# Hybrid RG-LRU layer on one core: the lead-in taken by pairs of contraction tiles, with all eight x_lru tiles in it

## The chip, the core and the metric

One core of a Trainium2 chip runs the whole kernel. Its engines work side by side and meet through semaphores: PE (TensorE) multiplies matrices, DVE (VectorE) and ACT (ScalarE) do elementwise work, POOL (GpSimd) and SP (SyncE) here mostly issue DMA transfers. The metric is device time in microseconds (us), lower is better. Matrix operands lie in SBUF with 128 partitions; products are summed in PSUM, which has eight banks of 512 float32 columns.

## The reference

One layer with two streams, 128 context tokens and 256 latent tokens, which the kernel carries together as T = 384 columns; D = 2048, LRU width 1024, eight heads of 128.

```python
m   = silu(cvec) @ w_mod + b_mod                 # six vectors of 2048: shift, scale, gate, shift, scale, gate
hn  = rmsnorm(x, g[0]) * (1.0 + mod[:, 1]) + mod[:, 0]
z   = hn @ w_in                                  # x_lru | y_gate | b_g | c_g | v, 1024 columns each
xc  = dwconv(x_lru, cw, (2, 1)) + cb             # four taps
o_f, s_f = rglru_dir(xc, ..., reverse=False)     # gates: block-diagonal 128x128 products, then a scan
o_b, s_b = rglru_dir(xc, ..., reverse=True)
lru_out = (o_f + o_b) * gelu(y_gate)
sc_out  = b_g * dwconv(c_g * v, sc_w, (1, 1))
x = x + mod[:, 2] * (concat(lru_out, sc_out) @ w_out)
hn = rmsnorm(x, g[1]) * (1.0 + mod[:, 4]) + mod[:, 3]
x = x + mod[:, 5] * ((silu(hn @ w_gate) * (hn @ w_up)) @ w_down)
```

The outputs are both streams after a final RMSNorm and the last states of the context scans.

## The kernel before, in words

Every float32 product is made of three matmuls of rounded operands (`product`): high activation by high weight, low activation by high weight, high activation by low weight. ACT rounds a weight block to its high part, DVE subtracts to get the low part, and four slots (`w_hi`, `w_lo`) hold such blocks. Weights arrive through four raw buffers `raw` of 1 MB. A contraction tile `k` is one of the 16 groups of 128 input channels; `KT` is 16.

The lead-in is what has to happen before `hn @ w_in` can run at full depth:

- **Rows of w_mod.** Shift and scale together are 4096 columns of `w_mod`. PE multiplies them with the two conditioning vectors in rows of 512 columns: four units of 1 MB each (`lead_matmuls`), summed in `MOD_BANK`. DVE copies a row to `mod_row` (`copy_lead_row`), PE turns it into columns (`turn_lead_row`), DVE adds the bias (`add_lead_bias`). Before, a row holds either the shift or the scale of four contraction tiles: rows 0, 2, 4 are shift, rows 1, 3, 5 scale. The last four tiles have one shift row and two scale rows of two tiles each (256 columns), nine rows in all (`LEAD_ROWS`). Only after both rows can four tiles be scaled.
- **Activations.** With 1/rms known (`make_rstd`), DVE makes the normalized tiles of a pair (`hat_pair`), DVE and ACT scale and shift the context and latent columns (`scale_ctx`, `norm_pair`), ACT rounds to `act_hi`, DVE makes `act_lo` (`low_act`).
- **x_lru in the lead-in.** SP loads, for each `k`, the first 768 columns of `w_in` (`load_x_weights`, two buffers `x_raw`); ACT and DVE split them (`round_x`, `subtract_x`). `x_product` is half of one `k`: three of six output tiles, each summed over all 16 `k` in a PSUM bank of its own (`X_BANKS`). The halves stand between the units of the later rows.
- **After it.** The other two x_lru tiles are a step of four blocks (`N_X3`, 4 us of PE each) with four of the units of a further w_mod row behind its blocks (`mod_units`). ACT copies finished x_lru tiles into `padded` (`pad_tile`), DVE convolves them (`convolve_x`), some of them in this step and the rest in the first of eight steps of `gm_step`, which also hold the gates of one head each (`head_gates`). Each step has eight blocks of eight products.
- **SP's order** is one queue: a w_mod unit waits until the matmuls have freed its raw buffer (`mod_used`), an x weight load until the low part made from its buffer is there (`lo_ready`). A load that waits holds up all loads behind it.

The instruction order of each engine is the order of the code; nothing is scheduled by a planner. `decays()` is a chain of 17 small DVE instructions on the decay parameters, placed between low parts 2, 3 and the first row of the loop over fours.

Of the kernel before, what the change touches and what calls it, by code (L numbers as in the profile page):

```python
# [23 lines left out]
ALU = mybir.AluOpType  # L24
# [4 lines left out]
P = 128  # L29
SLOTS = 4  # L30
# [33 lines left out]
def build(nc, x_prompt, x_sample, state_rglru, c, c_ctx, w_mod, b_mod, norm_g, w_in, lru_conv_w, lru_conv_b,  # L64
# [65 lines left out]
    N_X3 = KT  # L130
    N_IN = N_X3 + 4
    N_OUT = N_IN + (IN_STEPS - 2) * 8
    MOD_IN, MOD_OUT = MOD_FIRST + 1, MOD_FIRST + IN_STEPS - 1
    assert MOD_STEPS - MOD_FIRST == 1 + (IN_STEPS - 2) + OUT_STEPS + 3 and len(LEAD_UNITS) == 4 * MOD_FIRST
# [11 lines left out]
    with ExitStack() as ctx:  # L146
# [52 lines left out]
        x_squares = [lru[:, b] for b in (2, 3)]  # L199
        x_sumsq = scratch[:, 8 * T:10 * T].rearrange("p (a t) -> p a t", a=2)  # L200
# [4 lines left out]
        x_raw = [scratch[:, at:at + X_WIDE] for at in (4 * P + 8 * 2 * HEADS, 8 * T + 4 * PADDED + 2 * T - X_WIDE)]  # L205
        POS = GRID_ROWS * (KT // 2) + GRID_W * (KT // 2)
        pos = scratch[:, 8 * T + 2 * T:8 * T + 2 * T + POS]
# [7 lines left out]
        X_BANKS = (2, 3, 0, 1, 4, 5)  # L215
# [60 lines left out]
        x_pair_done = sem("x_pair_done")  # L276
        squared = sem("squared")
# [70 lines left out]
        def landings(kind, n, block):  # L348

            if kind in ("GM", "GX"):  # L350
                return X_LANDED + 16 * (block // 4 + 1) + 4 * (n - N_X3)
            earlier = 0 if block // 2 % 2 else 4 * (N_G1 - N_X3)
            return X_LANDED + earlier + 16 + 2 * (n - N_G1)

        X_LANDED = 16 * MOD_FIRST
# [59 lines left out]
        def gains_before(pair):  # L415

            return sum(1 for first, _ in LEAD_ROWS if KT <= first <= KT + 2 * pair)

        def lead_unit(row, unit):

            number = LEAD_UNITS.index((row, unit))
            slot = number % SLOTS
            width = P * LEAD_ROWS[row][1]
            return slot, 16 * (number // SLOTS + 1), raw[slot][:].rearrange("p (k n) -> p k n", n=width)
# [5 lines left out]
        def _(sp):  # L430
# [26 lines left out]
            def load_lead_unit(number):  # L457

                row, unit = LEAD_UNITS[number]
                first, tiles = LEAD_ROWS[row]  # L460
# [1570 lines left out]
```

## Time and profile before

| what | value |
|---|---|
| runs | 1747.32 us median of 3 (1746.41 to 1747.57) |
| profiled execution | span 1746.0 us from first to last instruction; its own total is not shown apart from that |
| PE busy | 1712.1 us, 98% of the span |
| DVE busy | 945.4 us, 54% |
| ACT busy | 610.0 us, 35% |
| HBM read | 303.55 MB, 176 GB/s over the span |

The lead-in is in the first 4 of 40 slices of 43.65 us of the page. PE is busy 5 tenths of the first slice and 9 or more of every other but the last. The DMA row reads 9, 9, 9, 6 there, and 3 to 8 in nearly all later slices. "PEclk" or "granted clock" is the TensorE clock in parts of full speed: 1.00 is 2.4 GHz and 0.50 is 1.2 GHz. A busy interval of a matmul holds its fill and drain, and neighbours overlap; how fast a stream runs is read from the distance between starts.

### The profile page before, as it was taken

The page shows a single profiled execution, that of the slowest core. Times are in us where ns is not written, and L with a number is a line of the kernel's source. Part 1 is how long each engine was busy: PE and PEld are TensorE (multiplying, and loading weights), DVE is VectorE, ACT ScalarE, POOL GpSimd, SP SyncE. Part 2 cuts the span into 40 slices and gives each one's busy share as a digit, 9 for nine tenths or more (in the row PEclk, how much of TensorE's full clock was granted, in tenths as well). Part 3 has the DMA queues.
Part 4 walks back from the last instruction along what each step waited for, and adds up shares of the span by engine and source line. Part 5 has one row for each costly group of instructions (what it writes and reads, how often), then busy time and mean ns, then how long its engine had stood idle before and what let it go on. Part 6 is the DMA issues. An engine that isn't in the chain of part 4 may idle for free.

```text
span 1746.0 us, 24522 instructions
## 1 busy us (share of the span) xinstructions
PE 1712.1 (98%) x10063; PEld 1634.1 (94%) x10063; DVE 945.4 (54%) x1405; ACT 610.0 (35%) x701; POOL 63.6 (4%) x99
## 2 busy tenths in 40 slices
PE   5999999999999999999999999999999999999997
PEld 3678999999999979999999999999999999999997
DVE  4447578777778578353535444353534435353445
ACT  3233555456522253223232322223222232223235
POOL 2000100110010110000000000000000000000000
PEclk8999999999999999999999999999999999999998
DMA  9996755676677876343334333433343334333421
GB/s 364 388 349 223 247 200 199 205 241 205 212 256 260 280 265 220 130 134 121 120 128 136 120 120 127 137 120 120 127 137 120 120 126 138 120 120 126 138 73 73
DMA packets 206269, 307.56 MB, mean 176 GB/s; under 512 B 5501, under 2 KB 151217, under 8 KB 203777
## 3 DMA queue, kind: packets, MB, share of 16 engines
q1 hardware_dynamic: 189472, 237.07, 40.5%
q0 software_dynamic: 16528, 69.63, 11.2%
q8 instruction: 43, 0.70, 0.2%
q14 instruction: 18, 0.14, 0.0%
q10 hardware_dynamic: 208, 0.02, 0.0%
HBM read 303.55 MB, written 3.15 MB: 176 GB/s over the span
## 4 chain that ended last, share of the span: by engine, by line
PE 93%; DMA 4%; DVE 1%; ACT 1%; SPq 0%; issue 0%; ACTq 0%; DVEq 0%
PE psum L1590 30%; PE psum L1591 29%; PE psum L1592 29%; DMA raw<-in_w_mod 2%; DMA scratch<-in_w_in 2%; PE psum L1620 1%; PE psum L1612 1%; PE psum L1634 1%; PE psum L1928 0%; PE psum L1645 0%; PE psum L1699 0%; ACT scratch L668 0%; DVE act_lo L1143 0%; DVE w_lo L1121 0%; SPq L465 0%
## 5 line engine op out<-in xcount | busy, mean ns | idle before, releaser
L971 DVE TENSOR_TENSOR w_lo<-raw,w_hi 128x1024 fp32r<-128x1024 f32 x364 | 444.1, 1224 | 643.3 <-ACT w_hi L633 642.9
L1590 PE MATMUL psum<-act_hi,w_hi 128*128 128x384 f32 x2240 | 753.8, 337 | 3.1 <-DVE act_lo L1143 2.3
L1592 PE MATMUL psum<-act_hi,w_lo 128*128 128x384 f32 x2240 | 750.2, 335 | 0.0
L1591 PE MATMUL psum<-act_lo,w_hi 128*128 128x384 f32 x2240 | 750.0, 335 | 0.0
L633 ACT ACTIVATE w_hi<-raw 128x1024 fp32r<-128x1024 f32 x364 | 381.6, 1058 | 790.9 <-PE psum L1592 717.1
L1590 PEld LDWEIGHTS psum<-act_hi,w_hi 128*128 128x128 f32 x2240 | 421.1, 188 | 26.3 <-issue 17.5
L1591 PEld LDWEIGHTS psum<-act_lo,w_hi 128*128 128x128 f32 x2240 | 421.3, 188 | 0.0
L1592 PEld LDWEIGHTS psum<-act_hi,w_lo 128*128 128x128 f32 x2240 | 421.2, 188 | 0.0
L1590 PE MATMUL psum<-h_hi,w_hi 128*128 128x384 f32 x768 | 258.3, 336 | 0.9 <-DVE h_lo L1450 0.9
L1592 PE MATMUL psum<-h_hi,w_lo 128*128 128x384 f32 x768 | 257.0, 335 | 0.0
L1591 PE MATMUL psum<-h_lo,w_hi 128*128 128x384 f32 x768 | 256.9, 335 | 0.0
L1590 PEld LDWEIGHTS psum<-h_hi,w_hi 128*128 128x128 f32 x768 | 144.2, 188 | 6.2 <-issue 5.0
L1591 PEld LDWEIGHTS psum<-h_lo,w_hi 128*128 128x128 f32 x768 | 144.3, 188 | 0.0
L1592 PEld LDWEIGHTS psum<-h_hi,w_lo 128*128 128x128 f32 x768 | 144.2, 188 | 0.0
L1459 DVE SCALAR_TENSOR_TENSOR xT<-psum,modT,xT 128x128 f32<-128x128 f32 x352 | 122.0, 409 | 6.8 <-PE psum L1592 6.7
L992 DVE SCALAR_TENSOR_TENSOR token_rows<-raw,cond,token_rows 128x512 f32<-128x512 f32 x90 | 61.6, 745 | 0.0
L1634 PE MATMUL psum<-raw,cond_w 128*32 128x512 f32 (+1 forms) x288 | 36.9, 602 | 5.7 <-DMA raw<-in_w_mod 5.6
L992 DVE SCALAR_TENSOR_TENSOR scratch<-stage,cond,scratch 128x512 f32<-128x512 f32 x62 | 42.4, 745 | 0.0
L870 ACT ACTIVATE h_hi<-stage 128x768 fp32r<-128x768 f32 x22 | 18.6, 847 | 51.6 <-DVE stage L1445 51.6
L827 ACT ACTIVATE scratch<-xT 128x768 f32 (+1 forms) x8 | 6.8, 847 | 77.7 <-DVE xT L1387 77.7
L1121 DVE TENSOR_TENSOR w_lo<-scratch,w_hi 128x768 fp32r<-128x768 f32 x16 | 15.1, 955 | 28.7 <-ACT w_hi L654 28.7
L654 ACT ACTIVATE w_hi<-scratch 128x768 fp32r<-128x768 f32 x16 | 13.3, 838 | 41.2 <-DMA scratch<-in_w_in 41.2
(191 smaller groups left out, 760.5 us busy)
## 6 DMA issues: line engine op xcount, KB each, us to landing
raw<-in_w_mod POOLq DMA_DIRECT2D x50, 1024.0 KB, 6.0
raw<-in_w_gate SPq DMA_DIRECT2D x44, 1024.0 KB, 5.0
raw<-in_w_up SPq DMA_DIRECT2D x44, 1024.0 KB, 5.0
raw<-in_w_down SPq DMA_DIRECT2D x44, 1024.0 KB, 4.9
raw<-in_w_in SPq DMA_DIRECT2D x34, 1024.0 KB, 5.3
raw<-in_w_mod SPq DMA_DIRECT2D x32, 1024.0 KB, 9.6
raw<-in_w_out SPq DMA_DIRECT2D x16, 1024.0 KB, 5.5
stage<-in_w_mod POOLq DMA_DIRECT2D x14, 1024.0 KB, 7.5
```

The lines of the kernel that those rows point to most:

```text
L633: act.activation(split_view(w_hi, b), source, ACT.Copy).then_inc(hi_ready, 1)
L870: act.activation(h_hi[:, 2 * pair:2 * pair + 2, :], silu_g[:, 2 * pair:2 * pair + 2, :], ACT.Copy)\
L971: dve.tensor_tensor(split_view(w_lo, b), source, split_view(w_hi, b).bitcast(F32), ALU.subtract).then_inc(lo_ready, 1)
L992: dve.scalar_tensor_tensor(sums[:, a, :], rows[:, j, :], cond[:, a, k:k + 1], sums[:, a, :], ALU.mult, ALU.add).then_inc(side_step, 1)
L1121: dve.tensor_tensor(w_lo[k % SLOTS][:, 0:X_WIDE], x_raw[k % 2], w_hi[k % SLOTS][:, 0:X_WIDE].bitcast(F32), ALU.subtract).then_inc(lo_ready, 1)
L1459: last = dve.scalar_tensor_tensor(xT[:, k, start:end], psum[:, down_banks[j] + a, start:end], modT[:, 5 * KT + k, seg:seg + 1], xT[:, k, s ...
L1590: pe.matmul(psum[:, bank, 0:T], hi, x_hi, start=first, stop=False)
L1591: pe.matmul(psum[:, bank, 0:T], hi, x_lo, start=False, stop=False)
L1592: return pe.matmul(psum[:, bank, 0:T], lo, x_hi, start=False, stop=last)
L1612: out = pe.matmul(psum[32 * j:32 * j + 32, MOD_BANK, :], cond_w[:, k, :], rows[:, 512 * j:512 * j + 512], start=k == 0, stop=k == KT - 1, ...
L1620: out = pe.matmul(psum[32 * j:32 * j + 32, MOD_BANK, :], cond_w[:, 4 * q + j, :], rows[:, j, :], start=q == 0, stop=q == 3, tile_position= ...
L1634: out = pe.matmul(psum[32 * j:32 * j + 32, MOD_BANK, 0:tiles * P], cond_w[:, depth * unit + i, :], rows[:, i, :], start=unit == 0 and i < ...
```

## The change

- **Rows.** There are eight rows of 512 columns; row r holds the shift of tiles 2r and 2r+1 in its first 256 columns and their scale in its last 256. Each 1 MB unit is now loaded by two DMAs of 512 KB, whose runs in HBM are 256 columns (1 KB) where they were 512 columns (2 KB). One row makes one pair of tiles ready.
- **x_lru.** All eight tiles are in the lead-in: 1024 columns of `w_in` for each `k`. Tiles 0 to 3 are summed over all `k` in banks 0 to 3 (`held_products`). Tiles 4 to 7 are summed in banks 4 and 5 over the two `k` of a pair only (`part_products`), and DVE adds each result to a sum in SBUF (`add_part`, 32 times; it copies in the first pair). The step `N_X3` is gone.
- **Order.** A row's four units stand together on PE, then two part products of the pair before, the turn of the row, and the rest of the pair's products. The convolutions and the first gates move into the first `gm_step`: `head_gates(0, 0)` and two mod units come after its block 1.
- **Loads.** The first row's units are issued ahead of the first two x weight loads. Scratch buffers move accordingly.

```diff
+    X_TILES = HEADS
+    X_HELD = X_TILES // 2
+    LEAD_COUNT = KT // 2
+    X_PART_BANKS = (4, 5)
...
+            def load_lead_unit(row, unit):
+                if row:
+                    sp.wait_ge(mod_used, 4 * row + unit - 3)
+                for s in range(2):
+                    at = s * D + 2 * P * row
+                    sp.dma_start(lead_unit(unit)[:, :, 2 * P * s:2 * P * s + 2 * P],
+                                 w_mod_v[:, 4 * unit:4 * unit + 4, at:at + 2 * P]).then_inc(landed[unit], 16)
...
+            for row in range(1, LEAD_COUNT):
+                load_lead_unit(row, 0)
+                load_lead_unit(row, 1)
+                load_x_weights(2 * row)
+                load_lead_unit(row, 2)
+                load_lead_unit(row, 3)
+                load_x_weights(2 * row + 1)
...
+            def add_part(pair, r):
+                seq = X_HELD * pair + r
+                if seq + 1 < X_HELD * (KT // 2):
+                    dve.wait_ge(part_done, seq + 1)
+                else:
+                    dve.wait_ge(block_done, KT)
+                source = psum[:, X_PART_BANKS[r % 2], 0:T]
+                if pair == 0:
+                    dve.tensor_copy(x_part(r), source).then_inc(part_added, 1)
+                else:
+                    dve.wait_ge(part_added, seq - X_HELD + 1)
+                    dve.tensor_tensor(x_part(r), x_part(r), source, ALU.add).then_inc(part_added, 1)
...
             decays()
+            for pair in range(1, KT // 2):
+                copy_lead_row(pair)
+                add_part(pair - 1, 0)
+                add_part(pair - 1, 1)
+                add_lead_bias(pair)
+                scale_ctx(pair)
+                low_act(pair)
+                add_part(pair - 1, 2)
+                add_part(pair - 1, 3)
+                if pair + 1 < KT // 2:
+                    hat_pair(pair + 1)
+                    subtract_x(2 * pair + 2)
+                    subtract_x(2 * pair + 3)
...
+            for row in range(1, LEAD_COUNT):
+                before = row - 1
                 for unit in range(4):
                     lead_matmuls(row, unit)
+                part_products(before, 0)
+                part_products(before, 1)
                 turn_lead_row(row)
+                held_products(2 * before)
+                part_products(before, 2)
+                part_products(before, 3)
+                held_products(2 * before + 1).then_inc(block_done, 1)
+            held_products(KT - 2)
+            part_products(KT // 2 - 1, 0)
+            part_products(KT // 2 - 1, 1)
+            held_products(KT - 1)
+            mod_units(0, 2)
+            part_products(KT // 2 - 1, 2)
+            part_products(KT // 2 - 1, 3)
```

`part_products(pair, r)` is two products (the two `k` of the pair) of tile 4 + r; `held_products(k)` is four products, one for each held tile.

SP's queue from its start to the fourth x weight load; `raw<-in_w_mod` is a unit of a lead row and `scratch<-in_w_in` an x weight load. Before:

```order
L455 DMA scratch<-in_w_in 128x768 x2
L465 DMA raw<-in_w_mod 128x4x512 x8
L455 DMA scratch<-in_w_in 128x768
L465 DMA raw<-in_w_mod 128x4x512 x2
L455 DMA scratch<-in_w_in 128x768
```

After:

```order
L461 DMA raw<-in_w_mod 128x4x256 x8
L453 DMA scratch<-in_w_in 128x1024 x2
L461 DMA raw<-in_w_mod 128x4x256 x4
L453 DMA scratch<-in_w_in 128x1024
L461 DMA raw<-in_w_mod 128x4x256 x4
L453 DMA scratch<-in_w_in 128x1024
```

Eight half units make one row, and the x weights are wider; from here on each row comes with two x weight loads, the second behind the last unit of the row.

DVE around the turn of row 1, from the low parts of x weights 2 and 3 to the copy of the next row; `w_lo` is such a low part, the `decay` and `scratch 128x16` rows are `decays()`, `mod_row` the copy that PE's turn waits for. Before, this is behind the second turn; `act_lo` makes pairs 0 and 1 ready:

```order
L1045 COPY mod_row<-psum 128x512 [waits mod_used]
L1052 TENSOR_TENSOR modT<-psum,prm 128x8 [waits row_turned]
L1060 SCALAR_TENSOR_TENSOR gain<-modT,prm 128x8 [waits mod_ready]
...
L1143 TENSOR_TENSOR act_lo<-scratch,act_hi 128x768 [waits act_hi_ready] x2
L1121 TENSOR_TENSOR w_lo<-scratch,w_hi 128x768 [waits hi_ready] x2
L1153 TENSOR_SCALAR scratch<-scratch 128x16 [waits prm_ready,exp_lam_ready]
...
L1164 TENSOR_SCALAR decay<-scratch 128x16 x2
L1121 TENSOR_TENSOR w_lo<-scratch,w_hi 128x768 [waits hi_ready]
L1045 COPY mod_row<-psum 128x512 [waits mod_used]
```

After:

```order
L1141 TENSOR_TENSOR act_lo<-scratch,act_hi 128x768 [waits act_hi_ready]
L1125 TENSOR_TENSOR stage<-xT,token_rows 128x768
L1120 TENSOR_TENSOR w_lo<-scratch,w_hi 128x1024 [waits hi_ready] x2
L1165 TENSOR_SCALAR scratch<-scratch 128x16 [waits prm_ready,exp_lam_ready]
...
L1176 TENSOR_SCALAR decay<-scratch 128x16 x2
L1044 COPY mod_row<-psum 128x512 [waits mod_used]
L1154 COPY stage<-psum 128x384 [waits part_done] x2
L1053 TENSOR_TENSOR modT<-psum,prm 128x2x4 [waits row_turned]
L1059 SCALAR_TENSOR_TENSOR gain<-modT,prm 128x4 [waits mod_ready]
```

The copy of row 1 was ahead of these low parts and of `decays()`, and is now behind both.

## Rows read from the trace of the kernel before

**Rows 1.** Windows: engines' busy us (and instructions), PE clock, DMA share, GB/s

```profile
60.00:100.00 40.00, 36.86 (x235) 23.29 (x237) 17.55 (x32) 12.39 (x18) 0.00 (x0) 1.00 1.05 389
...
121.00:142.00 21.00, 21.00 (x123) 20.82 (x122) 14.52 (x25) 10.76 (x21) 0.00 (x0) 1.00 0.50 172
```

**Rows 2.** Waits of PE over the whole span: us in total, times, longest

```profile
PE psum L1634 <- DMA raw<-in_w_mod: 5.6, 6, 1.7
...
PE psum L1645 <- DVE mod_row L1045: 2.2, 4, 0.8
```

**Rows 3.** Timeline of PE, lead-in: start us, us, operation

```profile
25.78 1.86 PE L1634 MATMUL psum<-raw,cond_w 128*32 128x512 f32 x8 [1.66 <-DMA raw<-in_w_mod]
...
44.02 0.69 PE L1590 MATMUL psum<-act_hi,w_hi 128*128 128x384 f32 x1 [0.70 <-DVE act_lo L1143]
...
45.14 0.52 PE L1590 MATMUL psum<-act_hi,w_hi 128*128 128x384 f32 x1
...
46.10 0.52 PE L1590 MATMUL psum<-act_hi,w_hi 128*128 128x384 f32 x1
...
83.35 1.06 PE L1634 MATMUL psum<-raw,cond_w 128*32 128x512 f32 x8
...
88.90 2.12 PE L1634 MATMUL psum<-raw,cond_w 128*32 128x512 f32 x16
...
108.03 0.95 PE L1645 MATMUL psum<-select,mod_row 128*128 128x2 f32 x8
108.90 1.07 PE L1634 MATMUL psum<-raw,cond_w 128*32 128x256 f32 x16
```

**Rows 4.** DMA view of 92 to 100 us, and of 104 to 106 us

```profile
DMA packets 1507, 3.11 MB, mean 389 GB/s; under 512 B 53, under 2 KB 53, under 8 KB 1507
...
DMA packets 696, 0.70 MB, mean 349 GB/s; under 512 B 14, under 2 KB 696, under 8 KB 696
```

**Rows 5.** Windows: first inputs, slow and rising clock, 1 KB pieces

```profile
8.00:10.00 2.00, 0.18 (x1) 0.18 (x1) 0.00 (x0) 0.00 (x0) 0.00 (x0) 1.00 1.05 404
...
43.00:44.00 1.00, 0.32 (x4) 0.00 (x0) 0.96 (x1) 0.97 (x3) 0.00 (x0) 0.50 1.02 388
...
49.00:50.00 1.00, 1.00 (x7) 0.94 (x4) 0.84 (x5) 0.00 (x0) 0.00 (x0) 0.59 1.05 397
...
110.00:112.00 2.00, 2.00 (x17) 1.66 (x21) 0.43 (x1) 0.84 (x1) 0.00 (x0) 1.00 1.10 351
```

**Rows 6.** Timeline of PE: row 1's units, a turn, end of the x_lru part

```profile
33.24 5.39 PE L1634 MATMUL psum<-raw,cond_w 128*32 128x512 f32 x32
...
67.88 1.05 PE L1645 MATMUL psum<-select,mod_row 128*128 128x2 f32 x8 [0.61 <-DVE mod_row L1045]
...
152.46 2.24 PE L1612 MATMUL psum<-raw,cond_w 128*32 128x512 f32 x16
...
155.78 0.33 PE L1590 MATMUL psum<-act_hi,w_hi 128*128 128x384 f32 x1
```

**Rows 7.** Timelines of ACT and DVE

```profile
65.39 0.84 ACT L654 ACTIVATE w_hi<-scratch 128x768 fp32r<-128x768 f32 x1 [6.00 <-DMA scratch<-in_w_in]
...
35.23 1.81 DVE L1127 TENSOR_TENSOR stage<-xT,token_rows 128x768 f32<-128x768 f32 x2
...
48.25 0.17 DVE L1153 TENSOR_SCALAR scratch<-scratch 128x16 f32<-128x16 f32 x1 [0.68 <-ACT scratch L714]
...
51.48 0.33 DVE L1164 TENSOR_SCALAR decay<-scratch 128x16 f32<-128x16 f32 x3
...
132.37 0.48 DVE L1263 TENSOR_SCALAR scratch<-scratch,prm 128x386 f32<-128x386 f32 x1 [2.37 <-ACT scratch L734]
...
134.86 0.48 DVE L1263 TENSOR_SCALAR scratch<-scratch,prm 128x386 f32<-128x386 f32 x1
```

**Rows 8.** The page: 1024-column weight splits; a 1 MB load with the queue empty

```profile
L971 DVE TENSOR_TENSOR w_lo<-raw,w_hi 128x1024 fp32r<-128x1024 f32 x364 | 444.1, 1224 | 643.3 <-ACT w_hi L633 642.9
L633 ACT ACTIVATE w_hi<-raw 128x1024 fp32r<-128x1024 f32 x364 | 381.6, 1058 | 790.9 <-PE psum L1592 717.1
...
raw<-in_w_down SPq DMA_DIRECT2D x44, 1024.0 KB, 4.9
```

More of the change, by code:

```diff
@@ L413, in late_before, with lead_unit @@
             return earlier[-1] if earlier else None
[L415 to L424, printed above, removed]
+        def lead_unit(unit):
+            return raw[unit][:].rearrange("p (k n) -> p k n", n=512)
         block_ctx = ctx.enter_context(nc.Block())
@@ L783, in _ @@
                     last.then_inc(gates_read, 1)
-                round_blocks("GM", n, range(3, 6))
+                if head == 0:
+                    for b in (4, 5):
+                        round_blocks("GM", n, range(b, b + 1))
+                        pad_tile(b + 1)
+                else:
+                    round_blocks("GM", n, range(3, 6))
                 if phase == "y":
@@ L1065, in make_gain @@
+                dve.wait_ge(gain_ready, row + 1)
             def make_gain(which, scale):
@@ L1624, in lead_matmuls @@
             def lead_matmuls(row, unit):
-                tiles = LEAD_ROWS[row][1]
-                slot, landing, rows = lead_unit(row, unit)
                 if row and unit == 0:
                     pe.wait_ge(row_ready, row)
-                pe.wait_ge(landed[slot], landing)
-                depth = rows.shape[1]
-                for i in range(depth):
-                    j = i % 4
-                    out = pe.matmul(psum[32 * j:32 * j + 32, MOD_BANK, 0:tiles * P], cond_w[:, depth * unit + i, :],
-                                    rows[:, i, :], start=unit == 0 and i < 4, stop=unit == tiles - 1 and i >= depth - 4,
-                                    tile_position=(0, 32 * j))
-                out.then_inc(mod_used, 1)
+                pe.wait_ge(landed[unit], 32 * (row + 1))
+                mod_matmuls(unit, lead_unit(unit))
             def turn_lead_row(row):
@@ L1643, in turn_lead_row @@
                     pe.wait_ge(mod_ready, row)
-                for a in range(LEAD_ROWS[row][1]):
+                for a in range(4):
                     out = pe.matmul(psum[:, SMALL_BANK, 2 * a:2 * a + 2], mod_row[:, a * P:(a + 1) * P], select[:, 0:2],
@@ L1726, in gm_step @@
                     if j == 0:
-                        if gates is not None:
+                        if gates is not None and (pair or gates_first):
                             gates(pair)
```

302 lines of the change are left out of this document (118 added, 184 removed).

## The prediction

> **What bounds the kernel now.** I read the page's slices first: PE is full everywhere but at the start, so a change of the lead-in can only win or lose there. Second the windows by stage. From 60 to 100 us the DMA engines are saturated, 389 GB/s at a share of 1.05, while PE is busy 36.9 of 40 us; from 121 to 142 us PE is busy all the time and the DMA only half of it [rows 1]. So the first 115 us or so are paced by transfers, with PE almost level, and what follows is PE alone. Third the waits of PE: 5.6 us on units of w_mod and 2.2 us on the copy of a row, none above 1.7 us [rows 2]. Fourth, the timeline: two rows with their products take from 83.35 to 108.90, 25.55 us [rows 3]. In that time come 8 units and 4 x weight loads, 8 x 1.049 + 4 x 0.393 = 9.96 MB, which at 389 GB/s is 25.6 us: the cycle is the DMA's. The first product starts at 44.02 [rows 3]; all of x_lru, four mod units and the gates of head 0 are done at 155.78 [rows 6]. That 155.78 is the mark that I compare; behind it both kernels do the same work with PE full.
>
> **The loads.** A pair now needs 4 units (4.194 MB) and two x weight loads of 1024 columns (1.049 MB). How fast is a unit in 1 KB runs? The trace has the case: the last two rows before are 256 columns wide. From 92 to 100 us, with runs of 2 and 3 KB, 3.11 MB go at 389 GB/s; from 104 to 106 us all 696 packets are under 2 KB, 0.70 MB, and go at 349 GB/s [rows 4], at a DMA share of 1.10 in the next such window, 351 GB/s [rows 5]. So I take 0.350 MB/us: 4.194/0.350 = 11.98 us, and 1.049/0.389 = 2.70 us for the x weights, 14.7 us a pair. The x weights may be a little quicker: inputs in 8 KB runs went at 404 GB/s [rows 5], 0.1 us less a pair.
>
> The Trainium skill, DMA: Bandwidth & Descriptors, section Specifications, gives 512 B as the least transfer at line rate. By that rule 1 KB runs cost nothing, and the result would be that of the second rival; the trace disagrees, 349 against 389 GB/s, with nearly every packet twice that size.
>
> **PE for one pair.** Four units at 2.12 us for two, 4.2; 16 products of three matmuls, with 123 matmuls in 21.0 us [rows 1] 0.171 each, 8.2; a turn 0.87 (108.03 to 108.90 [rows 3]); about 0.3 for the changes between kinds of matmul. Sum 13.6 us, so PE is quicker than the DMA by 1.1 us a pair. Before, the cycle for two rows was PE 8.5 + 6 x 4 x 0.51 = 12.3 + 1.8 and some 1.5 of changes, 24.1 against 25.6 on the DMA.
>
> **The start, step by step.** Row 0's last unit lands at 25.78 [rows 3]. Two x weight loads (0.79 MB, 2.0 us) go behind it and its four units cost 0.3 more each: 25.0. Then x weights 0, 1 (2.7): 27.7; row 1's units 0, 1 (6.0): 33.7; x weight 2: 35.0; units 2, 3: 41.0, against some 37.5 before (row 1's units end at 38.63, and one is 1.1 [rows 6]); x weight 3: 42.3. The pair's activation needs 1/rms, which is there at 35.2 where `hat_pair` starts [rows 7]: hat 0.9 and gain 0.2, scaling 1.1, rounding 0.85, low part 1.0, so 39.3. The products stand behind row 1's units, so they start at 42.1. That is 1.9 us earlier than 44.02, and not the 6 that one row in place of two seems to promise: the row is slower, and its x weights are in front of its last units.
>
> Then comes the first new wait. PE does two part products, 4 products at the slow clock (0.96 each, 45.14 to 46.10 [rows 3]), until 46.0, and turns row 1. The turn needs DVE's copy, which now stands behind x weight 3 and `decays()`: 42.3 + 1.06 + 0.2 for the absolute value + 1.3 table load + 0.3 = 45.2, then the chain of 3.56 us (48.25 to 51.81 [rows 7]) and the copy 0.7: 49.5. PE waits 3.5 us. Behind the turn on PE are 12 products of the pair. Nobody else is held up by that, except the next loads: row 3's units wait for row 2's matmuls.
>
> The clock was 0.50 from 43 us on and came back within 49 to 50 us, after 5.5 us of unbroken work [rows 5]. With the wait in between it can be 1.00 at once (then the 12 products and the turn take 7.1, to 56.7) or only after another 5.5 us (16 matmuls at 0.32, the rest at 0.171, with the turn 9.6, to 59.1). That is the value s, where row 2's units begin. The gap of 3.5 us looks like the idle stretch that had lowered the clock before, so I take the later one.
>
> **The DMA gap.** Row 2 and its x weights have landed at 42.3 + 14.7 = 57.0. Row 3's first unit is issued at s + 1.0, and about 2.1 us pass before bytes flow (a lone 1 MB load takes 4.9 us [rows 8], of which 2.7 to 3.0 is the transfer). The engines stand idle for 2.8 (s = 56.7) to 5.2 us (s = 59.1). From then on the loads stay ahead: a row's first unit is issued 1.0 us into the row before, when over 3 us of transfers are still under way. Each row's turn then waits some 1 us: x weight 2R+1 is the last to land, and its split (1.06 + 1.22) and the copy (0.65) stand before the turn, 2.97 us. (Before, 65.39 to 67.88 with 768 columns, 2.49 [rows 6, 7], plus 0.48 for 1024 columns [rows 8].) PE's own work up to the turn, four units and four products, ends earlier.
>
> **The sum.** The last x weight lands at 57.0 + gap + 5 x 14.7 = 133.3 to 135.7, less 0.6 if its runs go at 404. Behind it: 2.97, turn 0.9, 12 products of pair 6 (6.15), 16 products of pair 7 (8.2), two mod units 2.1, two more with gates 3.3 (152.46 to 155.78 [rows 6]), and 0.4 for changes and for block 1's low part, which comes 0.2 late (below). 24.0. So the mark stands at 156.7 to 159.7, against 155.78: +0.9 to +3.9. With the slow start +3.3 to +3.9, of which I take 0.1 off for faster small pieces: +3.2. On the profiled span that is 1746.0 + 3.2 = 1749.2; the median of the runs is 1.3 above the span, so 1750.5.
>
> **Costs put at nothing.** The 32 part sums on DVE: about 0.55 us each (0.69 for 512 columns in the copies), 2.2 a pair; DVE has per pair 0.7 + 2.2 + 0.3 + 0.6 + 1.0 + 0.9 + 2.4 = 8.1 us in 14.7. A part product waits for the sum two before it, which is 2 us or more old. Bounds: 0, or 0.5 a pair (4 us) if a sum stands behind a late x weight. The two DMAs in place of one cost SP 0.4 us an issue, under transfers. In the first gm step DVE has a convolution (2.49 us, 132.37 to 134.86 [rows 7]) and a low part (1.15 to 1.22) for each block of 4.1 us of PE. Block 1's low part comes behind the last sum and convolution 0: 0.6 + 2.5 + 1.2 = 4.3 after the last product, 0.2 late. The cover is thin: if it goes, this is the third rival.
>
> **Rivals.**
> - **A, the forecast.** DMA paced at 350 GB/s for the units. +1.5 to +5.
> - **B, the runs of 1 KB are as fast.** Then a pair is 13.5 us of DMA under 13.6 of PE. Row 1 lands at 38.6, x weight 3 at 40.0, row ready at 47.1, s = 54.3 to 56.7, then 6 x 13.6 and 8.2 + 5.4 + 0.4: the mark at 149.9 to 152.3, -5.9 to -3.5, so 1741.4 to 1743.8. For it: a lone load in 1 KB runs lands nearly as fast as one in 2 KB. Against it: both saturated windows [rows 4, 5].
> - **C, the clock is back at once or the gap is short.** PE's wait at the turn of row 1 doesn't slow the rest. Without any gap the mark is 130.5 - 0.6 + 24.0 = 153.9, -1.9; with the early s, +0.9 to +1.5. 1745.4 to 1748.8. For it: before, idle pieces of 0.8 us did not lower the clock; against it, this one is 3.5 us.
> - **D, DVE becomes the bound in the first gm step.** A convolution, a low part and a wait for the copy into `padded` per block: 2.49 + 1.15 + 0.5 (if ACT's copy cannot lie beside the convolution before it). From 4.1 us a block on PE waits; with 0.5 for each of 6 to 8 blocks, +3 to +4 on top of A: 1753.5 to 1755. For it: ACT's copies stand behind roundings that wait for PE. Against it: two buffers, and the same alternation before ran without a wait of PE.
>
> **How the numbers follow.** A 0.46, C 0.23, D 0.17, B 0.14. The measurement cannot tell less than 0.2%, 3.5 us, from no change: the borders are 1743.8 and 1750.8. A straddles the upper one, with 0.17 above; D is slower whole: 0.34. B is faster almost whole, with a little of C: 0.16. Same: 0.50. The range goes from the edge of B, 1743.5, to D's 1754; A's own is 1748.8 to 1752.5.
>
> **What would show it.** Right: 349 to 352 GB/s at a share near 1.1 while units of the lead-in land; a turn of row 1 that waits 3 us or more for `mod_row`, later turns about 1 us; an idle DMA of 3 to 5 us near 60 us; rows 14.7 us apart from row 3 on; the last product of x_lru at 155 to 157. Wrong: rows 13.6 apart with PE full (B), PE waits on `act_lo` or on part sums, or PE waits on `w_lo` for blocks 1 to 7 of the first gm step (D).

## The result, and the profile after

The kernel after takes 1758.97 us (median of the three runs at 1758.23 to 1759.65) against 1747.3 for the kernel before: ratio 1.0063, 95% interval 1.0047 to 1.0079. It is 11 to 12 us slower, where +3.2 was forecast in a range up to +6.7. A fourth run, 2425.4 us at a mean clock of 0.653, is left out; with it the median is 1759.31. The profiled execution is one of 1758.97 us, the middle of the three, with a span of 1757.2, 11.2 more than before.

The mark comes out of the timeline. In the kernel after, the gates of head 0 (172.22, below) and two mod units stand behind block 1, and block 2 starts at 175.21. Blocks 0 and 1 are 48 matmuls at 0.1735, 8.33 us, so the mark stands at 166.9, against 155.78 before [rows 6]: +11.1. All that was lost was lost ahead of the mark.

Timeline of PE in the kernel after, from row 0's last unit on (start us, us, operation, and in brackets the idle time before it and what ended it):

```profile
25.02 1.06 PE L1616 MATMUL psum<-raw,cond_w 128*32 128x512 f32 x8 [1.92 <-DMA raw<-in_w_mod]
...
39.98 1.93 PE L1616 MATMUL psum<-raw,cond_w 128*32 128x512 f32 x8 [3.16 <-DMA raw<-in_w_mod]
42.98 1.93 PE L1616 MATMUL psum<-raw,cond_w 128*32 128x512 f32 x8 [1.06 <-DMA raw<-in_w_mod]
44.84 0.69 PE L1586 MATMUL psum<-act_hi,w_hi 128*128 128x384 f32 x1
...
51.21 1.86 PE L1633 MATMUL psum<-select,mod_row 128*128 128x2 f32 x8 [3.30 <-DVE mod_row L1044]
52.94 0.67 PE L1586 MATMUL psum<-act_hi,w_hi 128*128 128x384 f32 x1
...
61.08 3.64 PE L1616 MATMUL psum<-raw,cond_w 128*32 128x512 f32 x32
...
78.89 1.07 PE L1616 MATMUL psum<-raw,cond_w 128*32 128x512 f32 x8 [1.81 <-DMA raw<-in_w_mod]
83.13 1.05 PE L1633 MATMUL psum<-select,mod_row 128*128 128x2 f32 x8 [0.89 <-DVE mod_row L1044]
...
112.34 1.05 PE L1633 MATMUL psum<-select,mod_row 128*128 128x2 f32 x8 [0.93 <-DVE mod_row L1044]
...
140.04 1.07 PE L1616 MATMUL psum<-raw,cond_w 128*32 128x512 f32 x8 [1.92 <-DMA raw<-in_w_mod]
144.31 1.05 PE L1633 MATMUL psum<-select,mod_row 128*128 128x2 f32 x8 [0.90 <-DVE mod_row L1044]
...
172.22 0.33 PE L1586 MATMUL psum<-h_hi 128*128 128x384 f32 x1
...
175.21 0.44 PE L1586 MATMUL psum<-act_hi,w_hi 128*128 128x384 f32 x1
```

These answer to [rows 3, 6]. Row 0 lands at 25.02 where 25.78 stood. Row 1's units then take 1.93 us each, in place of 1.07, because the clock is at 0.50 when they come; the first product starts at 44.84, later than before (44.02). The turn waits 3.30 us for the copy of row 1.

Waits of PE over the whole span (us in total, times, longest), against 5.6 and 2.2 us [rows 2]:

```profile
PE psum L1616 <- DMA raw<-in_w_mod: 11.9, 8, 3.2
...
PE psum L1633 <- DVE mod_row L1044: 7.8, 6, 3.3
```

Windows of the kernel after, for the same stretches as [rows 1] and then 1 KB pieces, the idle DMA near 60 us and some places further on (engines' busy us and instructions, clock, DMA share, GB/s):

```profile
60.00:100.00 40.00, 35.97 (x241) 25.75 (x240) 20.99 (x36) 9.68 (x12) 0.00 (x0) 1.00 0.97 324
121.00:142.00 21.00, 18.28 (x127) 11.74 (x126) 8.58 (x14) 4.73 (x6) 1.10 (x2) 1.00 1.04 346
...
52.00:54.00 2.00, 2.00 (x9) 2.00 (x9) 0.90 (x5) 0.43 (x1) 0.00 (x0) 0.50 1.10 348
...
56.00:58.00 2.00, 2.00 (x11) 2.00 (x10) 0.53 (x1) 0.00 (x0) 0.00 (x0) 0.83 0.43 166
58.00:60.00 2.00, 2.00 (x14) 2.00 (x13) 1.46 (x3) 1.06 (x1) 0.00 (x0) 1.00 0.01 2
60.00:62.00 2.00, 2.00 (x19) 1.15 (x21) 1.66 (x2) 0.76 (x1) 0.00 (x0) 1.00 0.00 0
62.00:64.00 2.00, 2.00 (x24) 0.61 (x20) 1.23 (x1) 0.30 (x1) 0.00 (x0) 1.00 0.23 64
...
74.00:76.00 2.00, 2.00 (x17) 0.42 (x16) 1.23 (x1) 0.03 (x1) 0.00 (x0) 1.00 1.10 346
...
108.00:110.00 2.00, 2.00 (x17) 1.11 (x14) 0.00 (x0) 0.64 (x1) 0.00 (x0) 1.00 0.91 275
110.00:112.00 2.00, 1.41 (x9) 1.08 (x7) 1.54 (x2) 0.42 (x1) 0.00 (x0) 1.00 0.92 297
...
116.00:118.00 2.00, 2.00 (x8) 2.00 (x8) 0.83 (x1) 0.00 (x0) 0.00 (x0) 0.50 1.09 356
...
122.00:124.00 2.00, 2.00 (x24) 0.60 (x20) 0.00 (x0) 0.00 (x0) 0.00 (x0) 1.00 0.78 267
...
146.00:148.00 2.00, 2.00 (x8) 2.00 (x7) 0.56 (x3) 1.78 (x3) 0.00 (x0) 0.50 1.06 429
```

From 121 to 142 us, where PE was full over a half idle DMA before, the DMA is now saturated (share 1.04) and PE is busy 18.28 of 21 us. The clock goes down to 0.50 again at 116 and at 146 us, with PE busy all the time in those windows: it shows as 8 matmuls in 2 us where a full window at full clock holds 12 or more. "PE full" in the busy column says nothing there.

Timeline of ACT in the kernel after, the split of the last x weight of rows 3 to 7, which starts when it lands:

```profile
80.16 1.06 ACT L657 ACTIVATE w_hi<-scratch 128x1024 fp32r<-128x1024 f32 x1 [6.13 <-DMA scratch<-in_w_in]
...
94.99 1.06 ACT L657 ACTIVATE w_hi<-scratch 128x1024 fp32r<-128x1024 f32 x1 [5.88 <-DMA scratch<-in_w_in]
...
109.36 1.06 ACT L657 ACTIVATE w_hi<-scratch 128x1024 fp32r<-128x1024 f32 x1 [5.42 <-DMA scratch<-in_w_in]
...
125.02 1.06 ACT L657 ACTIVATE w_hi<-scratch 128x1024 fp32r<-128x1024 f32 x1 [5.15 <-DMA scratch<-in_w_in]
...
141.33 1.06 ACT L657 ACTIVATE w_hi<-scratch 128x1024 fp32r<-128x1024 f32 x1 [6.26 <-DMA scratch<-in_w_in]
```

Distances 14.83, 14.37, 15.66, 16.31 us. The first two are the forecast's 14.7; the last two are longer by 1.0 and 1.6.

### The profile page after: what moved, and what is told of

Same layout as the page of the kernel before. It is cut to its first block, busy times and chain, and to the rows that moved or that the text cites. A ratio compares the mean times of both kernels' runs of the same rounds, so it can differ in the third digit from the quotient of the medians.

```text
span 1757.2 us, 24545 instructions
## 1 busy us (share of the span) xinstructions
PE 1713.1 (97%) x10031; PEld 1638.2 (93%) x10031; DVE 961.5 (55%) x1434; ACT 609.9 (35%) x697; POOL 63.5 (4%) x99
## 3 DMA queue, kind: packets, MB, share of 16 engines
q0 software_dynamic: 16528, 69.63, 11.1%
## 4 chain that ended last, share of the span: by engine, by line
PE 92%; DMA 3%; DVE 2%; SPq 2%; ACT 1%; issue 1%; ACTq 0%; DVEq 0%
PE psum L1586 30%; PE psum L1588 29%; PE psum L1587 29%; DMA scratch<-in_w_in 2%; PE psum L1616 1%; SPq L461 1%; PE psum L1608 1%; DMA select<-in_tables 0%; DVE token_rows L1198 0%; PE psum L1917 0%; PE psum L1633 0%; ACT w_hi L657 0%; PE psum L1687 0%; PE psum L1750 0%; SPq L453 0%
## 5 line engine op out<-in xcount | busy, mean ns | idle before, releaser
L971 DVE TENSOR_TENSOR w_lo<-raw,w_hi 128x1024 fp32r<-128x1024 f32 x360 | 439.3, 1224 | 634.6 <-ACT w_hi L636 634.0
L636 ACT ACTIVATE w_hi<-raw 128x1024 fp32r<-128x1024 f32 x360 | 377.3, 1058 | 785.9 <-PE psum L1588 711.1
L1616 PE MATMUL psum<-raw,cond_w 128*32 128x512 f32 x400 | 53.9, 640 | 11.9 <-DMA raw<-in_w_mod 11.9
L1616 PEld LDWEIGHTS psum<-raw,cond_w 128*32 128x32 f32 x400 | 9.8, 112 | 38.0 <-DMA raw<-in_w_mod 24.3
L1120 DVE TENSOR_TENSOR w_lo<-scratch,w_hi 128x1024 fp32r<-128x1024 f32 x16 | 19.5, 1222 | 32.4 <-ACT w_hi L657 32.4
L657 ACT ACTIVATE w_hi<-scratch 128x1024 fp32r<-128x1024 f32 x16 | 16.8, 1057 | 50.3 <-DMA scratch<-in_w_in 39.9
```

The lines of the kernel that those rows point to most:

```text
L636: act.activation(split_view(w_hi, b), source, ACT.Copy).then_inc(hi_ready, 1)
L971: dve.tensor_tensor(split_view(w_lo, b), source, split_view(w_hi, b).bitcast(F32), ALU.subtract).then_inc(lo_ready, 1)
L1120: dve.tensor_tensor(w_lo[k % SLOTS][:, 0:X_WIDE], x_raw[k % 2], w_hi[k % SLOTS][:, 0:X_WIDE].bitcast(F32), ALU.subtract).then_inc(lo_ready, 1)
L1616: out = pe.matmul(psum[32 * j:32 * j + 32, MOD_BANK, :], cond_w[:, 4 * q + j, :], rows[:, j, :], start=q == 0, stop=q == 3, tile_position= ...
```

## The experiments

Theories at the start: **1**, the 1 KB runs cost the difference, since the lead-in is paced by transfers; **2**, the new order costs it, by the waits at the turns and the slow clock behind them. All kernels were timed beside the kernel before (1747.65 us for the first four, 1747.83 for the next four, 1748.53 and 1747.63 for the last two). Each ratio is good to about 0.1%, 2 us. Below, the kernel after counts as 1758.97 us; differences between kernels are of medians, and one of 2 us is at the edge of what these runs tell. A second measure is the mark of the profiled execution, one execution of each kernel.

**The kernel before with 1 KB runs.** The rows of four tiles are loaded in two DMAs of 256 columns each; the narrower rows keep their 1 KB runs and are split in two as well, and the counts that wait for them follow.

```diff
-                sp.dma_start(to, w_mod_v[:, depth * unit:depth * unit + depth, first * P:(first + tiles) * P])\
-                    .then_inc(landed[slot], 16)
+                for part in range(2):
+                    if tiles == 4:
+                        cols = slice(2 * P * part, 2 * P * part + 2 * P)
+                        sp.dma_start(to[:, :, cols], w_mod_v[:, depth * unit:depth * unit + depth,
+                                                             first * P + 2 * P * part:first * P + 2 * P * part + 2 * P])\
+                            .then_inc(landed[slot], 16)
...
```

> The kernel before, with one thing changed: each 1 MB unit of the first seven lead rows is loaded by two DMAs whose runs are 1 KB (256 columns) where they were 2 KB; same bytes, same place. Theory 1, the size of the runs sets the pace of the lead-in: 28 units cost 3.0 in place of 2.7 us, 8.4 us in all, and the DMA paced the lead-in already, so +6 to +9 us, 1753 to 1756. Theory 2, the new order (copy of a row behind low parts, part sums on DVE) makes the loss and the loads have slack: 0 to +2 us, 1747 to 1749.

Measured 1757.58 us, ratio 1.0056 (1.0043 to 1.0069): +9.9 us, more than theory 1 gave. Its waits of PE and one window:

```profile
PE psum L1643 <- DMA raw<-in_w_mod: 10.2, 8, 2.1
PE psum L1654 <- DVE mod_row L1054: 3.4, 4, 1.4
PE psum L1599 <- DVE act_lo L1152: 2.9, 3, 1.2
...
60.00:100.00 40.00, 34.31 (x218) 21.30 (x218) 14.09 (x23) 8.73 (x12) 0.00 (x0) 1.00 1.09 356
```

356 GB/s at a share of 1.09 stands where 389 at 1.05 stood [rows 1], and the first product starts 4.0 us later (48.07 against 44.02). Order, turns and x weights are those of before. The edit does two things, shorter runs and two DMAs for a unit; the kernels of fours below, with two DMAs for a unit and 2 KB runs, reach 389 to 392 GB/s where their queue is full, so it is the length of the runs.

**The kernel after with 2 KB runs.** Each unit is loaded as two halves of 512 neighbouring columns. Shift and scale then come from the wrong columns.

```diff
-                    at = s * D + 2 * P * row
-                    sp.dma_start(lead_unit(unit)[:, :, 2 * P * s:2 * P * s + 2 * P],
-                                 w_mod_v[:, 4 * unit:4 * unit + 4, at:at + 2 * P]).then_inc(landed[unit], 16)
+                    at = 4 * P * row
+                    sp.dma_start(lead_unit(unit)[:, 2 * s:2 * s + 2, :],
+                                 w_mod_v[:, 4 * unit + 2 * s:4 * unit + 2 * s + 2, at:at + 4 * P]).then_inc(landed[unit], 16)
```

> The changed kernel with units loaded in 2 KB runs: 512 neighbouring columns of w_mod, two DMAs for each unit as in the changed kernel, so shift and scale of a pair are taken from other columns than the reference wants. Theory 1: a pair's loads take 13.5 us in place of 14.7 (8 rows, about 9.5 us less), PE is then as slow as the DMA: 1744 to 1750. Theory 2: the order makes the loss: 1756 to 1759.

Measured 1752.3 us, ratio 1.0028 (1.0018 to 1.0038). So the 1 KB runs are worth 6.7 us in the new order, and the new order is 4.7 us slower than before even without them. That is above theory 1's range and below theory 2's: both hold a part. The turn of row 1 still waits 3.34 us:

```profile
48.83 1.05 PE L1633 MATMUL psum<-select,mod_row 128*128 128x2 f32 x8 [3.34 <-DVE mod_row L1044]
```

**Row 1's copy first.** On DVE the copy goes ahead of x weight 3's low part, which follows it, and of `decays()`, which goes behind the activations of pair 1.

```diff
-            subtract_x(3)
-            decays()
             for pair in range(1, KT // 2):
                 copy_lead_row(pair)
+                if pair == 1:
+                    subtract_x(3)
                 add_part(pair - 1, 0)
...
                 low_act(pair)
+                if pair == 1:
+                    decays()
```

> The changed kernel with DVE's copy of row 1 ahead of x weight 3's low part and of the decay chain, which moves behind the activation of pair 1. Theory 1: PE's wait of 3.3 us at the turn of row 1 goes, with a slow stretch of the clock behind it, and row 3's loads start that much earlier: row 2's units begin 3.5 to 5 us earlier, 1754 to 1756. Rival: the loads have the same end anyway (they wait for something else): 1758 to 1759.5.

Measured 1752.51 us, ratio 1.0029 (1.0017 to 1.0041): 6.5 us back, for a wait of 3.30, and more than theory 1 gave. The mark comes at 159.0 (gates at 164.31) in place of 166.9, 7.9 us earlier. The window that holds it, to be read against the idle DMA of 56 to 63 us above:

```profile
44.00:60.00 16.00, 16.00 (x105) 12.20 (x98) 10.95 (x32) 6.72 (x9) 0.00 (x0) 0.94 1.05 344
```

PE has no wait in it, the clock is 0.94 on average and the DMA gap is all but gone. The wait costs about twice its length: the clock is low behind it, the next row's units start later, and for that time the DMA has nothing to do.

**Every row's copy first.** In addition, the copy of each later row goes ahead of the low part of the x weight that lands last.

```diff
                 copy_lead_row(pair)
-                if pair == 1:
-                    subtract_x(3)
                 add_part(pair - 1, 0)
                 add_part(pair - 1, 1)
+                subtract_x(2 * pair + 1)
...
                     subtract_x(2 * pair + 2)
-                    subtract_x(2 * pair + 3)
```

> As the run with row 1's copy ahead, and every later row's copy too is ahead of the low part of the x weight that lands last (2R+1), which moves behind the row's first two part sums. Theory 1: the waits of 0.8 to 1.0 us at turns 3 to 7 come back partly as waits on units, since the loads set the pace, but the two falls of the clock near 115 and 145 us (1.7 us each) and the late loads behind the first of them go: 2 to 4 us less than that run, 1750 to 1753. Rival, the turns' waits cost nothing: the same as that run.

Measured 1750.14 us, ratio 1.0015 (1.0006 to 1.0023): another 2.4 us, at the edge of what the runs tell (this kernel's own spread over 6.9 us), but the trace bears it out. PE waits for no copy any more, and in the lead-in its clock stays at 1.00 from about 49 us on, where the run with row 1's copy first still had it at 0.50 from 94 to 96 us. What is left is a clean picture of a DMA-paced lead-in, here each row's last unit:

```profile
73.53 1.07 PE L1616 MATMUL psum<-raw,cond_w 128*32 128x512 f32 x8 [1.92 <-DMA raw<-in_w_mod]
88.12 1.07 PE L1616 MATMUL psum<-raw,cond_w 128*32 128x512 f32 x8 [1.37 <-DMA raw<-in_w_mod]
102.77 1.06 PE L1616 MATMUL psum<-raw,cond_w 128*32 128x512 f32 x8 [1.45 <-DMA raw<-in_w_mod]
117.39 1.06 PE L1616 MATMUL psum<-raw,cond_w 128*32 128x512 f32 x8 [1.42 <-DMA raw<-in_w_mod]
132.03 1.07 PE L1616 MATMUL psum<-raw,cond_w 128*32 128x512 f32 x8 [1.43 <-DMA raw<-in_w_mod]
```

14.6 us apart, with 1.4 us of waiting in each: what PE would finish in 13.2 waits for 14.6 of transfers. The gates stand at 161.46, the mark 5.3 ahead of them (172.22 - 166.9 above) at 156.1: 2.9 us earlier than with row 1's copy first, and only 0.3 behind the kernel before. The span is 1.7 longer than before. The rest lies far behind the lead-in, in a stretch that both kernels have near 615 us; before, and then in this kernel:

```profile
605.00:635.00 30.00, 29.67 (x194) 22.16 (x193) 22.81 (x43) 17.11 (x25) 4.49 (x6) 0.94 0.71 245
...
605.00:635.00 30.00, 29.99 (x187) 21.49 (x186) 21.74 (x39) 16.66 (x24) 4.51 (x6) 0.89 0.67 235
```

A clock of 0.89 in place of 0.94 over 30 us is 1.5 us of work. Six of the profiled executions, before and after among them, have the short slow stretch there, five have the long one and one (the kernel after with 2 KB runs) has none. So the time of one execution carries up to 2 us that have nothing to do with the lead-in; what decides between the cases is not settled by these runs.

**Both: every copy first and 2 KB runs.** The two edits together, again with shift and scale from the wrong columns.

```diff
-                    at = s * D + 2 * P * row
+                    at = 4 * P * row
...
+                subtract_x(2 * pair + 1)
...
-                    subtract_x(2 * pair + 3)
```

> Both edits together: every row's copy first, and units in 2 KB runs (shift and scale of a pair from other columns than the reference wants). Theory 1: this is the prediction's second rival, 13.5 us of loads under 13.6 us of PE for a row, no waits at turns and no fall of the clock: 1742 to 1746, and at least 4 us under the run with the copies first, which has the same order and only slower units. Theory 2 (the loads have slack once the copies are first): within 1 us of that run, 1749 to 1750.5.

Measured 1742.32 us, ratio 0.9966 (0.9952 to 0.9979), 7.8 us below the one with 1 KB runs. That is the time of the prediction's rival B, 1741.4 to 1743.8. The fit is a little lucky: the gates stand at 154.37, so the mark is at 149.1 where B had 149.9 to 152.3, and 1.2 us of that are lost again near 610 us. PE is busy 38.08 of 40 us, and the DMA is faster by 22 GB/s than with 1 KB runs (359 in that kernel):

```profile
60.00:100.00 40.00, 38.08 (x254) 28.49 (x253) 21.69 (x38) 12.19 (x15) 0.00 (x0) 1.00 1.03 381
```

**Row 2's units between the products of pair 0** (on top of every copy first), which frees raw buffers earlier and should close the DMA's gap near 57 us.

```diff
-                for unit in range(4):
-                    lead_matmuls(row, unit)
+                if row != 2:
+                    for unit in range(4):
+                        lead_matmuls(row, unit)
...
                 held_products(2 * before)
+                if row == 1:
+                    lead_matmuls(2, 0)
                 part_products(before, 2)
...
```

> The run with all copies first, with row 2's four units between the products of pair 0, so that row 3's loads are issued before row 2's have all landed. Theory 1: the idle stretch of the DMA near 57 us (2 us) goes, rows stay 14.65 apart, so every later row and the end come 2 us earlier: 1747.5 to 1748.5. Rival, PE's own work sets the end: 1750.

Measured 1748.28 us, ratio 1.0003 (0.9994 to 1.0012): 1.9 us less. The window of 58 to 60 us is full, where the run with all copies first has 153 GB/s from 56 to 58 and 279 from 58 to 60 (that run, then this one):

```profile
58.00:60.00 2.00, 2.00 (x20) 0.88 (x9) 2.00 (x4) 1.06 (x1) 0.00 (x0) 1.00 0.91 279
...
58.00:60.00 2.00, 2.00 (x15) 0.91 (x14) 1.58 (x2) 0.94 (x1) 0.00 (x0) 1.00 1.10 348
```

Its rows come 1 us earlier than without the edit (131.02 for row 7's last unit against 132.03, gates at 160.46 against 161.46), and still 14.6 apart. So the trace shows half of the 1.9 us.

**Narrower x weights** (on top of every copy first): from `k` = 2 on only 768 of the 1024 columns are loaded, so tiles 6 and 7 are not the reference's; all arithmetic stays.

```diff
-                sp.dma_start(x_raw[k % 2], w_in_v[:, k, 0:X_WIDE]).then_inc(x_w_landed[k % 2], 16)
+                sp.dma_start(x_raw[k % 2][:, 0:X_WIDE if k < 2 else 768], w_in_v[:, k, 0:X_WIDE if k < 2 else 768]).then_inc(x_w_landed[k % 2], 16)
```

> The run with all copies first, with x weight loads of 768 columns in place of 1024 from the third on (the last 256 columns keep old values, so the x_lru tiles 6 and 7 are not those of the reference). 14 x 0.131 MB less. Theory 1, the loads set the pace of each row: 0.67 us a row, 4 to 5 us less than the run with the copies first, to PE's limit: 1745 to 1746.5. Rival: PE's order sets it: within 1 us of that run.

Measured 1746.41 us, ratio 0.9992 (0.9983 to 1.0001): 3.7 us less. 14 x 0.131 MB are 1.84 MB, 4.7 us at 389 GB/s. In the profiled execution the gates stand at 160.26, only 1.2 us earlier than without the edit; there the clock falls once more, behind a unit wait of 1.93 us, and the loads behind it come late:

```profile
70.00:80.00 10.00, 8.06 (x47) 6.14 (x44) 3.22 (x7) 1.06 (x1) 0.00 (x0) 0.83 1.09 358
80.00:90.00 10.00, 10.00 (x70) 7.12 (x69) 5.14 (x8) 4.06 (x5) 0.00 (x0) 1.00 0.89 290
```

**Fours again, with all eight x_lru tiles.** A version meant to beat both kernels: rows of 2 KB runs, shift or scale of four tiles as before; all eight x_lru tiles as after; copies early; products two rows behind the units; the units of even rows stand between products, those of odd rows together.

```diff
-                    at = s * D + 2 * P * row
+                    at = row % 2 * D + 4 * P * (row // 2)
...
-            for row in range(1, LEAD_COUNT):
-                before = row - 1
+            for row in range(2, LEAD_COUNT + 1):
+                before = row - 2
...
```

> A version meant to beat both: eight lead rows in 2 KB runs as before (shift or scale of four contraction tiles), all eight x_lru tiles in the lead-in with four in banks and four as part sums, DVE's copies first, products two rows behind. Whole result. Theory 1: it starts as late as before (44 us), but needs neither 1 KB runs nor waits for late rows: PE nearly full from 44 us on, rows 13.6 apart, 1740 to 1745. Rival: the loads of 10.5 MB for two rows (27.0 us) hold it as they hold the changed kernel: 1746 to 1750.

Measured 1746.38 us, ratio 0.999 (0.9981 to 0.9999): 1.4 us less than before, not the 3 to 8 of theory 1, and at the lower end of the rival's range. The profile shows the clock at 0.68 from 60 to 70 us, behind unit waits of 1.39 and 1.61, and the DMA at 292 GB/s behind that:

```profile
60.00:70.00 10.00, 7.00 (x35) 3.85 (x28) 4.31 (x8) 1.37 (x2) 0.00 (x0) 0.68 1.05 392
70.00:80.00 10.00, 10.00 (x65) 8.31 (x64) 7.03 (x13) 5.53 (x8) 0.00 (x0) 0.98 0.80 292
```

**Units between products in the odd rows too.** The edit also puts DVE's copy of an odd row behind the first two part sums, and the turn behind the third part product.

```diff
-                        for unit in range(4):
-                            lead_matmuls(row, unit)
+                    lead_matmuls(row, 0)
                     part_products(before, 0)
+                    lead_matmuls(row, 1)
                     part_products(before, 1)
+                    lead_matmuls(row, 2)
                     held_products(2 * before)
+                    lead_matmuls(row, 3)
...
-                    copy_lead_row(row)
                     add_part(before, 0)
                     add_part(before, 1)
+                    copy_lead_row(row)
```

> The kernel of fours, with one edit: in its odd rows too the four units stand one by one between products (unit 0, two products, unit 1, two products, unit 2, four products, unit 3, two products, turn, the rest), where they stood together ahead of all products. In the kernel of fours the profile had unit waits of 1.4 and 1.6 us inside row 3's units, then 12 matmuls at 0.32 us each in place of 0.17 at the slow clock (1.9 us), and a dip of the DMA to 292 GB/s from 70 to 80 us, because row 4's loads were issued late. Theory 1 (a unit that lands late costs only its own wait if products stand between the units, and the clock stays up): no slow clock between 50 and 120 us, DMA at 385 to 392 GB/s from 60 to 110 us, gates of head 0 at 155.5 to 158 in place of 160.0, so 1742 to 1744.5. Rival (the transfers pace the rows anyway, so waits only move): unit waits add up to 5 us or more as before, gates at 159.5 or later, 1746 or more.

Measured 1749.7 us, ratio 1.0005 (0.9996 to 1.0014). That is 3.3 us above the last one, of which 0.7 go with the kernel before beside it (1748.53 against 1747.83). The time is the rival's, but theory 1's mechanism is there:

```profile
60.00:70.00 10.00, 10.00 (x65) 6.72 (x64) 6.10 (x11) 1.41 (x2) 0.00 (x0) 1.00 1.05 392
70.00:80.00 10.00, 9.17 (x60) 6.35 (x59) 6.12 (x11) 5.35 (x8) 0.00 (x0) 1.00 1.05 391
...
132.96 0.66 PE L1613 MATMUL psum<-act_hi,w_hi 128*128 128x384 f32 x1 [2.69 <-DVE stage L1163]
```

Clock and DMA are full and PE waits for no unit behind 50 us, but part sums on DVE now stand behind the activations' low parts, and PE waits for them: 0.83, 0.83 and 2.69 us. The last of these is followed by a window at a clock of 0.83 (130 to 140 us).

**The same with DVE and ACT put in order for it.**

```diff
+                if row == KT // 2 - 1:
+                    round_x(2 * row)
...
+                    subtract_x(2 * row - 1)
                     copy_lead_row(row)
-                    subtract_x(2 * row - 1)
+                    add_part(before, 2)
                     add_lead_bias(row)
...
                     low_act(row - 1)
+                    add_part(before, 3)
                     low_act(row)
-                    add_part(before, 2)
-                    add_part(before, 3)
```

> The kernel of fours with units between products, with DVE and ACT reordered in the odd rows: x weight 2R-1's low part ahead of the copy of the row, the third part sum right behind the copy, the fourth between the two low parts of the activations; in the last row ACT rounds x weight 14 ahead of the two pairs. Its forerunner's profile had the clock at 1.00 from 50 to 130 us and the DMA at 386 to 392 GB/s, as hoped, and yet the time did not move: PE waited 0.83, 0.83 and 2.69 us for part sums that stood behind the low parts of the activations, and the last x weight was issued at 126.9 us only. Theory (the gain was turned into these waits): no wait for a part sum over 0.3 us, the last x weight issued by 123 us, the 4.4 us come back nearly whole: 1744 to 1746.5, ratio 0.9975 to 0.9990. Rival (the rows are paced by the transfers up to 125 us, and the waits are only what is left over): the waits go to units or to the last x weight, 1747.5 or more.

Measured 1746.94 us, ratio 0.999 (0.9981 to 0.9999). The waits for part sums are gone, PE is busy 40 of 40 us from 60 to 100 us, the last x weight is issued at 122.67 us, and the gates come at 158.96 in place of 161.72:

```profile
60.00:100.00 40.00, 40.00 (x254) 27.64 (x254) 24.20 (x47) 9.96 (x14) 0.00 (x0) 1.00 1.04 389
```

Just above its range in time, inside it in ratio. It is level with the first version of fours. Both are the best kernels of this study that compute the reference's result, 0.1% under the kernel before, at the edge of what can be told from no change. The lead-in itself won more: the mark is at 153.7, 2.1 us ahead of before, but the span is only 0.6 less, since this execution has the long slow stretch near 615 us (0.89 from 605 to 635). PE is full but for 1.46 us at 131.40 and the first 50 us, where two rows have to land before the first product (47.33 us). No run here tries to shorten that start.

## Why the prediction was wrong

**Most of the mechanism was the forecast's.** 1 KB pieces went at 346 to 348 GB/s at a share of 1.10, rows were 14.6 apart once the waits were out (14.7 forecast), the turn of row 1 waited 3.30 (3.5), the later turns 0.80 to 0.96 ("about 1 us"), row 0 landed at 25.02 (25.0). Rival D did not come: in the first `gm_step` PE waited for no low part. The run with every copy first has its mark at 156.1; the prediction's sum without a gap was 153.9 (rival C), and that run still has a short one (153 GB/s from 56 to 58 us).

**What failed is the size: the mark is 7.9 us above the forecast's 159.0.** Going down the steps:

1. *"units 2, 3: 41.0 ... x weight 3: 42.3 ... products start at 42.1."* Measured 42.98 (start of the last unit's matmuls), 44.29 (start of ACT's split) and 44.84: 2.0, 2.0 and 2.7 late. The step left out 0.26 MB of gate weights, which POOL's queue moves between 31 and 40 us (0.7 us), and it let row 1 have the DMA for itself, though row 2's first units go in beside its last loads. It also counted a unit at the full clock: the clock was 0.50 from 30 to 46 us, and each unit took 1.93 in place of 1.07.
2. *The wait at the turn, "PE waits 3.5 us".* Right: copy at 50.47, 6.2 behind x weight 3 (6.5 counted). But all of it comes 2 us later, so *s, "56.7 to 59.1"*, was 61.08. The step's choice of the later end held (clock 0.50 at 52.94, back at 56.8); it is step 1 that pushes it out.
3. *The gap of the DMA, "2.8 to 5.2".* The four windows from 56 to 64 us moved 0.46 MB where 350 GB/s would be 2.80: 6.7 us. Row 2 had landed when forecast, only s was late. Then *"rows 14.7 apart"* was counted from a row's first byte to its last x weight, but 5.84 MB moved from 64 to 80.2 us, not 5.24: the next row's units had been issued at 75.22 and took 0.6 MB, 1.7 us, in between. So the last x weight of row 3 lands at 80.16 where 57.0 + 5.2 + 14.7 = 76.9 was forecast: 3.3 us, 1.5 by the gap and 1.8 by this.
4. *"From then on the loads stay ahead"*, and turns that wait 1 us each at no further cost. That is where the reasoning failed, not only a number. PE's 13.6 us for a row and 0.9 of waiting at the turn leave almost nothing against the 14.7 of the loads, so the next row's units were issued late again and again (91.61, 106.45, 122.38) and the DMA fell below its rate: 275 and 297 GB/s from 108 to 112 us, 267 from 122 to 124. The second of these holes stands behind a slow clock as well: the 0.93 us wait at the turn was followed by 0.50 at 116 us, ten to twelve matmuls at 0.32 in place of 0.173, about 1.7 us. From 109.36 to 125.02 the DMA made 331 GB/s where it had made 352 in the two rows ahead: 1.0 us. In the last row, 125.02 to 141.33, it made 354, but 5.77 MB in place of 5.24: weights of the first `gm_step`, issued from 136.46 on, went in between, about 1.5 of its 1.6 us. The last two rows are 2.6 us more than 14.7 in sum by this, the two ahead of them 0.2 less. The prediction leaned on "before, idle pieces of 0.8 us did not lower the clock" (rival C). That did not always carry over.
5. *"Tail 24.0".* 166.9 - 141.33 = 25.5; the slow clock at 146 us is the 1.5. And the 0.6 for x weights at 404 GB/s did not come.

3.3 + 2.6 - 0.2 + 1.5 + 0.6 = 7.8: the miss of 7.9 is accounted for in the trace. The split within a step is read from one execution and not tested by a run of its own.

**From the experiments' side.** The waits for copies of a row cost 6.5 (row 1) and 2.4 us (the others), about 9 us together; by the marks 7.9 and 2.9. By the sum, row 1's wait was worth 3.5 to 5.2 (its length, or the 5.2 of the gap where the clock comes back with it), and the others nothing. The 1 KB runs cost 7.8 us (7.0 by the marks); rival B gave 6.8 to 7.4 for them (156.7 - 149.9 and 159.7 - 152.3), so this term was sized right. Without both, the new order is 5.5 us faster than the kernel before, inside rival B's sum. So the mis-sized term is the waits: row 1's was given 5.2 at most and the later ones nothing, where a wait in a stretch that the DMA paces costs its length, the slow clock that may follow it and the loads that are issued later.

**The page's rule** (the Trainium skill, DMA: Bandwidth & Descriptors, Specifications: 512 B is the least transfer at line rate) was put second to the trace in the prediction. The runs decide the same way: the same bytes in runs of 1 KB in place of 2 KB cost 9.9 us in the order of before and 6.7 and 7.8 in that of after, with 356 against 389 and 359 against 381 GB/s over 40 us.

## What to carry to other kernels

Where a stretch is paced by DMA, a wait of PE is priced not by its length alone: the clock may fall behind it, and a load may be issued later because of it; here a 3.3 us wait cost 6.5. Put what PE waits for (a copy of a row) ahead of everything on DVE that only the next stage needs. And before a layout cuts the runs of a saturated queue in half, read the rate of such runs from the trace: 10% of the rate was worth more (7.8 us) than the better order won over the kernel before (5.5).

## What the runs showed of the hardware

- In a saturated queue, windows with little but runs of 1 KB show 346 to 351 GB/s with the engines' share at 1.10, and 40 us of such units with wider x weights between them 356 to 359 with 1.08 to 1.09; units in runs of 2 KB show 381 to 392 with 1.03 to 1.05. The higher share with the lower rate is how it is seen.
- The clock has two levels in these traces, 1.00 (2.4 GHz) and 0.50 (1.2 GHz). It was low behind the 3.30 us at the turn of row 1, behind waits of 0.9 us at a turn (116 and 146 us in the kernel after, the latter 3 us behind a unit wait of 1.92 us), and behind 1.39 + 1.61 us within the units of one row (the first kernel of fours).
- The same waits did not always lower it. In the kernel after, 1.81 us for a unit and then 0.89 at the turn (78.89 and 83.13 us) left it at 1.00, and so did the turn waits of 0.96 and 0.80. A unit wait of 1.92 us at 73.53 left it at 1.00 (every copy first), and one of 1.93 at 73.18 was followed by 0.50 (narrower x weights). What sets these cases apart is not settled by these runs, so the price of a single short wait cannot be told ahead from them.
- A row's busy share hides the clock: PE is busy 2.00 of 2 us both with 8 matmuls at 0.50 and with 12 or more at 1.00. Counts of instructions tell.
